# Stick-breaking mixer reordered (v in q's banks), and the second block's layer norms by token block

## The chip, the cores and the metric

The kernel runs on one core of one Trainium2 chip. The metric is the device time of one execution in microseconds (us). The kernel below ("before") took 2758.28, 2760.16 and 2761.77 us in three runs, median 2760.16 us.

## The reference

256 tokens of 1024 features go through two blocks in float32. The first has two layers of FFN, mixer, FFN and gate; its mixer is stick-breaking attention in layer 0 and a pooling mixer in layer 1. The second has two layers of mixer, layer norm, PEER (each token's 128 of 16,384 experts), layer norm; its mixer is MLA in layer 0 and DSA (attention over keys that an indexer picks) in layer 1.

```python
def stick_breaking_attention(h, w_qkv, q_gain, k_gain, w_o):
    q, k, v = jnp.split(h @ w_qkv, 3, axis=-1)          # each 256 x 1024
    q = rms_norm(q.reshape(B, S, 16, 64), q_gain)       # per head
    k = rms_norm(k.reshape(B, S, 16, 64), k_gain)
    ...  # z = q k^T / 8; weights = exp(log_sigmoid(z) + later log_sigmoid(-z)); o = weights v
    return o @ w_o

def second_block(x, ...):
    for i in range(2):
        m = _mla_mixer(x, ...) if i == 0 else _dsa_mixer(x, ...)      # both end in o @ w_o
        x = _layernorm(DN_ALPHA * x + m, ln_gain[i, 0], ln_bias[i, 0])
        f = _peer(x, peer_w_q[i], peer_sub_keys[i], peer_w_down[i], peer_w_up[i])
        x = _layernorm(DN_ALPHA * x + f, ln_gain[i, 1], ln_bias[i, 1])
    return x
```

`_layernorm` takes mean and variance over a token's 1024 features: both column halves.

## The kernel before

**Tiling.** The tokens are two token blocks of 128 (`TB`), the features two halves of 512 columns (`HALVES`). A 256x1024 product is four parts (block, half), one PSUM bank each. `acc(0)` ("set 0") is banks 0 to 3, `acc(1)` banks 4 to 7. Weights come as units of 128x1024 (512 KB). SP loads a unit into a ring of six raw slots, ACT rounds it to `w_hi` (L655), DVE writes the rest `w_lo = raw - w_hi` (L1106), and PE makes three products for each part: high times high, high times low, low times high (L1848, L1849, L1850; `mm3`). A unit is 12 matmuls of 512 columns, a unit of the 584-wide indexer rows 6 of 512 and 6 of 72. `split(n)` on ACT or DVE is n such units; `unit_used` counts what PE has used, `hi_done` and `lo_done` what is ready. Activations are held turned (features on partitions) as `act_hi` and `act_lo` in `act_both`; PE turns rows with 128x128 transposes (L1880, L1891).

**Order.** Each engine's program is written by hand in one order, and waits are semaphores: `t.after(s)` counts the next value. `rows(set, n)` are n units into a set, `by_part` announces the last unit part by part.

**Stick-breaking mixer.** PE makes q's eight units into set 0 and k's into set 1, then turns q into banks 0 to 3 (L1880), waits until k is kept, makes v's units into set 1 and turns k after the sixth (`KEY_TURN`). ACT keeps q, k and v out of PSUM with their squares (`keep_acc`, L728). DVE scales q's and k's heads (`head_norm`, L1242), with splits after each. Then `stick_breaking` runs eight pairs of heads: logits (L1982), sums (L1991), mixing. `wo`'s eight units go to set 0.

**Layer norm of the second block.** `layer_norm` on DVE: four residual adds out of PSUM that also sum (L1351), a mean after each second (L1357), then for each block: wait for ACT's square (L831), variance (L1116), POOL's power (L488), scale by halves (L1372, two of 128x512). PE turns eight 128x128 per block; ACT scales the turned rows into `xT` and copies to `act_hi`, DVE subtracts into `act_lo` (L1140, `turned_ln`). Gain and bias are put on `x` itself later, by two DVE instructions per block: behind the experts' norm by `finish_x` (L1378, L1379), one split after the turning.

**Places.** The layer norm stands behind MLA's `wo` (before PEER's queries), behind the experts' down products (before DSA's indexer rows), behind DSA's `wo` (before the gather) and at the end; in the first two its last adds wait for the parts of the last unit, and a split stands behind it. Behind DSA's `wo` ACT squares both blocks first, then turns block 0 (`turned_whole`), block 0's first queries and scores follow on PE (`first_block`), DVE ranks them (L1566), and the gather begins.

**POOL's queue.** In layer 0 POOL scatters gates by 256 indirect DMAs (L544) and brings them back. In layer 1 it loads `pad` (gain and bias), makes the last 16 of the 128 copies of 512 KB that fill `both_rows` in DRAM (L567; both stand behind `x_changed(TB)`, a wait for both blocks of `finish_x`), and then gathers 256 times (L583); DVE takes the dot products (L1739), PE the weighted sums (L2294). SP's loads are queue q1 of the profile, POOL's q0.

## Time and profile before

| | us |
|---|---|
| median of three runs | 2760.16 (2758.28 to 2761.77) |
| the profiled execution | 2757.85 |
| its span | 2756.0 |
| PE busy | 2542.8 (92%) |
| DVE busy | 2062.0 (75%) |
| ACT busy | 1279.2 (46%) |
| POOL busy | 1147.6 (42%) |

The mean granted TensorE clock was 0.985 of full. Busy shares are averages over stages with different limits.

### The profile page before, as it was taken

The page shows a single profiled execution, that of the slowest core. Times are in us where ns is not written, and L with a number is a line of the kernel's source. Part 1 is how long each engine was busy: PE and PEld are TensorE (multiplying, and loading weights), DVE is VectorE, ACT ScalarE, POOL GpSimd, SP SyncE. Part 2 cuts the span into 40 slices and gives each one's busy share as a digit, 9 for nine tenths or more (in the row PEclk, how much of TensorE's full clock was granted, in tenths as well). Part 3 has the DMA queues.
Part 4 walks back from the last instruction along what each step waited for, and adds up shares of the span by engine and source line. Part 5 has one row for each costly group of instructions (what it writes and reads, how often), then busy time and mean ns, then how long its engine had stood idle before and what let it go on. Part 6 is the DMA issues. An engine that isn't in the chain of part 4 may idle for free.

```text
span 2756.0 us, 38867 instructions
## 1 busy us (share of the span) xinstructions
PE 2542.8 (92%) x12724; PEld 1980.0 (72%) x12724; DVE 2062.0 (75%) x4122; ACT 1279.2 (46%) x2160; POOL 1147.6 (42%) x1482
## 2 busy tenths in 40 slices
PE   8999899999999999999999899999987888887777
PEld 7887688878888877899999788887765333433223
DVE  7886588788878876798999567666777776777675
ACT  5555555555555555555555445455443222222222
POOL 4443044344434411388787533331103444444443
PEclk9999999999999999999999999999999999999998
DMA  9996799889979966455556799997938999999998
GB/s 356 379 320 211 283 384 373 279 328 377 324 264 383 368 222 218 153 175 182 183 180 198 250 382 389 383 385 285 314 129 341 422 416 422 412 422 419 414 411 341
DMA packets 217832, 873.30 MB, mean 317 GB/s; under 512 B 38320, under 2 KB 38448, under 8 KB 184048
## 3 DMA queue, kind: packets, MB, share of 16 engines
q0 software_dynamic: 118496, 511.47, 47.6%
q1 hardware_dynamic: 99072, 359.38, 37.0%
q10 hardware_dynamic: 144, 1.05, 0.1%
q8 instruction: 51, 0.84, 0.1%
q14 instruction: 69, 0.57, 0.1%
HBM read 786.70 MB, written 152.17 MB: 341 GB/s over the span
## 4 chain that ended last, share of the span: by engine, by line
PE 50%; DMA 21%; POOL 12%; DVE 7%; issue 5%; ACT 3%; SPq 0%; DVEq 0%; POOLq 0%; ACTq 0%
PE ps L1931 12%; DMA arena<-both_rows,arena 11%; POOL gate_cells L544 11%; PE ps L1848 8%; PE ps L1849 8%; PE ps L1850 8%; DMA both_rows<-in_stream 8%; PE ps L2294 6%; PE ps L1933 6%; DVE arena L1739 2%; PE ps L2251 1%; DMA raw<-in_stream 1%; DVE w_lo L1106 1%; PE ps L2032 1%; ACT w_hi L655 1%
## 5 line engine op out<-in xcount | busy, mean ns | idle before, releaser
L1106 DVE TENSOR_TENSOR w_lo<-raw,w_hi 128x1024 fp32r<-128x1024 f32 x665 | 811.0, 1223 | 290.4 <-ACT w_hi L655 285.8
L655 ACT ACTIVATE w_hi<-raw 128x1024 fp32r<-128x1024 f32 x665 | 701.8, 1058 | 461.0 <-DMA raw<-in_stream 316.3
L2294 PE MATMUL ps<-arena 128*128 128x512 f32 x1024 | 483.1, 620 | 126.5 <-ACT arena L872 126.4
L1931 PE MATMUL ps<-act_both,w_hi 128*128 128x512 f32 x1408 | 502.3, 399 | 6.6 <-DVE act_both L1134 4.8
L2294 PEld LDWEIGHTS ps<-arena 128*128 128x128 f32 x1024 | 192.8, 196 | 406.1 <-ACT arena L872 204.4
L1739 DVE SCALAR_TENSOR_TENSOR arena<-arena 128x1024 f32<-128x1024 f32 x256 | 313.6, 1225 | 186.6 <-DMA arena<-both_rows,arena 184.9
L583 POOL DMA_INDIRECT arena<-both_rows,arena x256 | 290.5, 1135 | 369.5 <-PE ps L2294 342.5
L516 POOL DMA_DIRECT2D both_rows<-arena x512 | 280.1, 554 | 353.1 <-DVE arena L1183 343.4
L1848 PE MATMUL ps<-w_hi,act_both 128*128 128x512 f32 (+1 forms) x990 | 386.0, 390 | 26.1 <-DVE w_lo L1106 12.8
L1933 PE MATMUL ps<-act_both,w_lo 128*128 128x256 f32 x1408 | 394.8, 280 | 0.0
L1849 PE MATMUL ps<-w_lo,act_both 128*128 128x512 f32 (+1 forms) x990 | 383.0, 387 | 0.0
L1850 PE MATMUL ps<-w_hi,act_both 128*128 128x512 f32 (+1 forms) x990 | 382.5, 387 | 0.0
L544 POOL DMA_INDIRECT gate_cells<-hot x256 | 316.0, 1235 | 110.2 <-issue 83.2
L1848 PE MATMUL ps<-act_both,w_hi 128*128 128x256 f32 x1192 | 339.5, 285 | 3.6 <-DVE act_both L1140 1.5
L1849 PE MATMUL ps<-act_both,w_hi 128*128 128x256 f32 x1192 | 338.0, 284 | 0.0
L1850 PE MATMUL ps<-act_both,w_lo 128*128 128x256 f32 x1192 | 337.9, 283 | 0.0
L1931 PEld LDWEIGHTS ps<-act_both,w_hi 128*128 128x128 f32 x1408 | 264.5, 188 | 74.9 <-issue 4.5
L1933 PEld LDWEIGHTS ps<-act_both,w_lo 128*128 128x128 f32 x1408 | 265.8, 189 | 3.0
L865 ACT ACTIVATE hot<-hot 128x2 f32<-128x2 f32 (+1 forms) x132 | 26.8, 203 | 458.3 <-DVE arena L1739 457.5
L1848 PEld LDWEIGHTS ps<-w_hi,act_both 128*128 128x128 f32 x990 | 188.1, 190 | 69.6 <-DVE w_lo L1106 12.0
L1848 PEld LDWEIGHTS ps<-act_both,w_hi 128*128 128x128 f32 x1192 | 229.4, 192 | 5.1 <-issue 3.8
L1849 PEld LDWEIGHTS ps<-act_both,w_hi 128*128 128x128 f32 x1192 | 229.5, 193 | 0.0
(276 smaller groups left out, 3652.8 us busy)
## 6 DMA issues: line engine op xcount, KB each, us to landing
raw<-in_stream SPq DMA_DIRECT2D x675, 512.0 KB, 3.4
arena<-in_stream POOLq DMA_DIRECT2D x128, 512.0 KB, 9.7
both_rows<-arena POOLq DMA_DIRECT2D x512, 128.0 KB, 6.3
both_rows<-in_stream POOLq DMA_DIRECT2D x128, 512.0 KB, 7.0
gate_cells<-hot POOLq DMA_DIRECT2D x32, 512.0 KB, 21.2
hot<-gate_cells POOLq DMA_DIRECT2D x128, 128.0 KB, 7.0
gate_cells<-hot POOLq DMA_INDIRECT x256
arena<-both_rows,arena POOLq DMA_INDIRECT x256, 10.8
```

Source lines behind the costliest of these rows:

```text
L516: pool.dma_start(rows.rearrange("(c r) k -> r c k", r=32), arena[32 * a:32 * a + 32, A_RELAY_OUT + UNIT * s:A_RELAY_OUT + UNIT * s + UNIT] ...
L544: pool.indirect_dma_start(gate_cells[:, :], bass.IndirectOffsetOnAxis(ap=cell[:, q:q + 1], axis=0), weights[:, q:q + 1], None).then_inc(sc ...
L583: pool.indirect_dma_start(row[:, p % ROW_RING, :], None, both_rows[:, :], at).then_inc(row_in[p % ROW_RING], 16)
L655: act.activation(w_hi[:, u % SPLIT, :], raw[:, u % RAW, :], ACT.Copy).then_inc(hi_done, 1)
L1106: dve.tensor_tensor(w_lo[:, u % RAW, :], raw[:, u % RAW, :], w_hi[:, u % SPLIT, :].bitcast(F32), ALU.subtract).then_inc(lo_done, 1)
L1739: dve.scalar_tensor_tensor(row[:, p % ROW_RING, 0:D], row[:, p % ROW_RING, 0:D], 1.0, x_rows[:, b, :], ALU.mult, ALU.mult, accum_out=dots[ ...
L1848: pe.matmul(dst, lhs[0], rhs[0], start=first, stop=False, **kw)
L1849: pe.matmul(dst, lhs[0], rhs[1], start=False, stop=False, **kw)
L1850: return pe.matmul(dst, lhs[1], rhs[0], start=False, stop=last, **kw)
L1931: pe.matmul(ps[:, bank, :], high, act_both[:, :, k, :], start=k == 0, stop=k == KD - 1, skip_group_check=True)
L1933: ins = pe.matmul(ps[:, bank, T:2 * T], low, act_hi[:, k, :], start=False, stop=k == KD - 1, skip_group_check=True)
L2294: ins = pe.matmul(ps[:, 2 * (n % 2) + half, :], diags[:, p % DIAG_RING, :], row[:, p % ROW_RING, D + 512 * half:D + 512 * half + 512], sta ...
```

## The change

In the stick-breaking mixer v's units stand directly behind k's and go to q's banks (set 0), the turns of q and k go to banks 4 to 7 and stand after v's second and seventh unit (`QUERY_TURN`, `KEY_TURN`), the pairs' banks are turned by four, and `wo` and the norm behind it change sets. ACT and DVE have two units fewer ahead of the pairs and two more among them.

In three of the four layer norms the last units (`TAIL` two, `DSA_TAIL` three behind DSA's `wo`) are made part by part rather than unit by unit (`last_units`): all of block 0 first. `layer_norm` on DVE starts block 0's variance before block 1's last add. Behind MLA's `wo`, ACT scales straight into `act_hi`, and DVE computes `xT` again from PSUM. Behind the experts, the first pair of turned features and the first two indexer units go by token block too, splits stand between the pairs, and `finish_x` is cut in two `finish_block`s: one five splits later, one behind the indexer's rope and two more splits. On POOL `x_changed(TB)` moves from behind the last `norm()` of layer 0's gates to ahead of `pad`'s load, with all of the layer's copies behind it that stood behind it before.

-KEY_TURN = 5
+QUERY_TURN, KEY_TURN = 1, 6
...
+TAIL, DSA_TAIL = 2, 3
@@ -609,6 +611,7 @@
         if i == 1:
+            x_changed(TB)
             pool.dma_start(pad[:, :], lnc[2 * i]).then_inc(ln_in, 16)
@@ -631,7 +634,6 @@
         norm()
-        x_changed(TB)
@@ -685,17 +687,36 @@
+    def scaled_pair(dst, n, pair, lo, hi):
+        act.wait_ge(turned, t.after(turned))
+        for k in (2 * pair, 2 * pair + 1):
+            g = G_LN + 2 * KD * n + k
+            ins = act.activation(dst[:, k, lo:hi], ps[:, 4 + pair, (k % 2) * T + lo:(k % 2) * T + hi],
+                                 ACT.Identity, scale=cst[:, g:g + 1], bias=cst[:, g + KD:g + KD + 1])
+        return ins
     def turned_ln(n):
...
+        for pair in range(4):
+            scaled_pair(act_hi, n, pair, 0, T).then_inc(turned_hi, 1)
+    def pair_high(pair, lo=0, hi=T):
+        both = slice(2 * pair, 2 * pair + 2)
+        act.activation(act_hi[:, both, lo:hi], xT[:, both, lo:hi], ACT.Copy).then_inc(turned_hi, 1)
...
+    def turned_ln_apart(n):
+        scaled_pair(xT, n, 0, 0, P).then_inc(first_pair_read, 1)
+        act.wait_ge(first_pair_read, 1)
+        pair_high(0, 0, P)
+        split()
+        step(scaled_pair(xT, n, 0, P, T))
+        pair_high(0, P, T)
+        for pair in range(1, 4):
+            step(scaled_pair(xT, n, pair, 0, T))
+            pair_high(pair)
+            split(2 if pair == 2 else 1)
@@ -803,6 +824,8 @@
             if p + 2 < N_PAIRS:
                 softplus(p + 2)
+            else:
+                split()
@@ -908,14 +931,14 @@
             keep_acc(q_tok, 0, roots=1)
-            split(KD)
-            keep_acc(k_tok, 1, roots=1)
-            keep_turned(area(A_QT, 2048), range(4), cst[:, QG:QG + 1])
-            split(KEY_TURN + 1)
-            keep_turned(area(A_KT, 2048), range(4), cst[:, KG:KG + 1])
+            split(KD - 1)
+            keep_acc(k_tok, 1, roots=1, pending=1)
+            split(3)
+            keep_turned(area(A_QT, 2048), range(4, 8), cst[:, QG:QG + 1])
+            split(KD - SPLIT)
+            keep_turned(area(A_KT, 2048), range(4, 8), cst[:, KG:KG + 1])
             act.preload_act_table_set("natural_log_exp_and_others")
-            split(KD - KEY_TURN - 1)
-            keep_acc(v_tok, 1, roots=1)
+            keep_acc(v_tok, 0, roots=1, pending=2)
@@ -1013,7 +1036,7 @@
-            split(KD)
+            split(KD - 3)
             keep_acc(tok(S_I, 584), 0, 584)
@@ -1035,19 +1058,18 @@
             split(KD - SPLIT)
-            layer_norm()
+            layer_norm([0])
             turned_whole(2 * i, 0)
+            layer_norm([1])
             first_block()
             turned_whole(2 * i, 1)
             gathered()
             layer_norm([1])
...
-        split(KD - 1)
+        split(KD - TAIL)
         layer_norm()
-        split()
         turned_ln(2 * i)
+        split(TAIL)
@@ -1082,9 +1104,8 @@
-        split(RING - 1)
+        split(RING - TAIL)
         layer_norm()
-        split()
@@ -1134,11 +1155,33 @@
+    def pair_low(pair, lo=0, hi=T):
+        both = slice(2 * pair, 2 * pair + 2)
+        dve.tensor_tensor(act_lo[:, both, lo:hi], xT[:, both, lo:hi], act_hi[:, both, lo:hi].bitcast(F32),
+                          ALU.subtract).then_inc(act_ready, 1)
+    def turned_ln(n):
+        for pair in range(4):
             dve.wait_ge(turned_hi, t.after(turned_hi))
-            dve.tensor_tensor(act_lo[:, 2 * b:2 * b + 2, :], xT[:, 2 * b:2 * b + 2, :],
-                              act_hi[:, 2 * b:2 * b + 2, :].bitcast(F32), ALU.subtract).then_inc(act_ready, 1)
+            for k in (2 * pair, 2 * pair + 1):
+                g = G_LN + 2 * KD * n + k
+                ins = dve.tensor_scalar(xT[:, k, :], ps[:, 4 + pair, (k % 2) * T:(k % 2) * T + T],
+                                        cst[:, g:g + 1], cst[:, g + KD:g + KD + 1], ALU.mult, ALU.add)
+            step(ins)
+            pair_low(pair)
+    def first_low():
+        dve.wait_ge(turned_hi, t.after(turned_hi))
+        pair_low(0, 0, P)
+    def turned_ln_apart():
+        split()
+        dve.wait_ge(turned_hi, t.after(turned_hi))
+        pair_low(0, P, T)
+        for pair in range(1, 4):
+            dve.wait_ge(turned_hi, t.after(turned_hi))
+            pair_low(pair)
+            split(2 if pair == 2 else 1)
@@ -1357,31 +1402,45 @@
+    def layer_norm(pending=1, first_at_once=False, between=None):
+        def summed(n):
             b, c = part(n, pending)
             residual(b, n % HALVES, c)
-            if n % HALVES == HALVES - 1:
-                mean(b)
-        dve.wait_ge(mean_ready, t.after(mean_ready, TB))
-        for b in range(TB):
+        def variance_of(b):
             dve.wait_ge(stat_ready, t.after(stat_ready))
-            inverse_root(b, small[:, 4 + b:5 + b], LN_EPS)
+            dve.tensor_scalar(small[:, b:b + 1], small[:, 4 + b:5 + b], 1.0 / D, LN_EPS, ALU.mult,
+                              ALU.add).then_inc(var_ready, 1)
+        def scale(b, between=None):
+            dve.wait_ge(mean_ready, t.after(mean_ready))
+            dve.wait_ge(rstd_ready, t.after(rstd_ready))
             for h in range(HALVES):
                 dve.tensor_scalar(x[:, b, half(h)], x[:, b, half(h)], small[:, 12 + b:13 + b],
                                   small[:, 16 + b:17 + b], ALU.add, ALU.mult).then_inc(rows_ready, 1)
+                if h == 0 and between is not None:
+                    between()
+        summed(0)
+        summed(1)
+        mean(0)
+        summed(2)
+        variance_of(0)
+        if first_at_once:
+            scale(0)
+        summed(3)
+        mean(1)
+        if not first_at_once:
+            scale(0)
+        variance_of(1)
+        scale(1, between)
-    def finish_x():
-        t.after(ln_in, 16)
@@ -1393,14 +1452,14 @@
             stick_terms()
-            head_norm(q_tok, 1.0, HD * EPS)
-            head_norm(k_tok, 1.0 / HD, EPS)
+            head_norm(q_tok, 1.0, HD * EPS, KD - 6)
+            head_norm(k_tok, 1.0 / HD, EPS, 2)
             t.skip(acc_kept)
...
                 b, c = part(n, 1)
-                dve.tensor_tensor(x[:, b, c], acc(0)[:, b, c], x[:, b, c], ALU.add).then_inc(x_ready, 1)
+                dve.tensor_tensor(x[:, b, c], acc(1)[:, b, c], x[:, b, c], ALU.add).then_inc(x_ready, 1)
@@ -1471,7 +1528,9 @@
-            split(KD)
+            split(KD - 3)
+            t.after(ln_in, 16)
+            finish_block(0, ln_in, t.value(ln_in))
@@ -1484,7 +1543,9 @@
             dve.tensor_copy(kid[:, :, IDX:P], kid[:, :, 0:IDX]).then_inc(rows_ready, 1)
-            split(KD)
+            split(2)
+            finish_block(1, ln_in, t.value(ln_in))
+            split(KD - 2)
@@ -1529,12 +1590,12 @@
             split(KD - SPLIT)
-            layer_norm(pending=SPLIT)
+            layer_norm(pending=SPLIT, first_at_once=True)
         else:
-            split(KD - 1)
-            layer_norm()
-            turned_ln()
-            split()
+            split(KD - TAIL)
+            layer_norm(pending=TAIL)
+            turned_ln(2 * i)
+            split(TAIL)
@@ -1828,8 +1889,8 @@
-        split(RING - 1)
-        layer_norm()
+        split(RING - TAIL)
+        layer_norm(TAIL, between=first_low)
@@ -1855,9 +1916,9 @@
+    def rows(set_, n_units, n=D, fresh=True, at=0, then={}, by_part=None, late=(), tail=0, skip=0):
...
             if k in then:
                 then[k]()
+        last_units([(at + k, unit()) for k in range(n_units - tail, n_units)], by_part, set_)
+    def last_units(pairs, by_part, set_=0, **kw):
+        for b in range(TB if pairs else 0):
+            for h in range(HALVES):
+                for n, (k, s) in enumerate(pairs):
+                    ins = mm3(ps[:, 4 * set_ + 2 * b + h, :], a(k, P * b, P), w(s, 512 * h, 512), False,
+                              n == len(pairs) - 1, **kw)
+                    if (b, h) == (TB - 1, HALVES - 1):
+                        ins.then_inc(unit_used, 1)
+                if (b, h) != (TB - 1, HALVES - 1):
+                    ins.then_inc(by_part, 1)
@@ -1886,6 +1960,8 @@
     def turn_block(b):
         for k in range(KD):
+            if (b, k) == (0, KD - HALVES):
+                pe.wait_ge(mean_ready, TB * (2 * DEPTH - 1))
             if k % (KD // HALVES) == 0:
@@ -1912,6 +1988,29 @@
+    def turn_first_pair_apart():
+        for b in range(TB):
+            for k in range(KD):
+                if k % (KD // HALVES) == 0:
+                    pe.wait_ge(rows_ready, t.after(rows_ready))
+                if (b, k) == (1, 0):
+                    pe.wait_ge(first_pair_read, 1)
+                ins = pe.transpose(ps[:, 4 + k // 2, T * (k % 2) + P * b:T * (k % 2) + P * b + P],
+                                   x[:, b, P * k:P * k + P], ident)
+                if k == 1 or (b and k % 2):
+                    ins.then_inc(turned, 1)
+    def first_units_apart(n):
+        s = [unit() for _ in range(TAIL)]
+        for b in range(TB):
+            pe.wait_ge(act_ready, t.after(act_ready))
+            for k in range(TAIL):
+                for lo in range(0, n, 512):
+                    m = min(512, n - lo)
+                    ins = mm3(ps[:, 2 * b + lo // 512, 0:m], a(k, P * b, P), w(s[k], lo, m), k == 0, False)
+                if b:
+                    ins.then_inc(unit_used, 1)
@@ -2071,20 +2170,22 @@
+            def turn_queries():
+                pe.wait_ge(acc_kept, t.after(acc_kept))
+                pe.wait_ge(rows_ready, t.after(rows_ready))
+                turn_rows(q_tok, range(4, 8))
             def turn_keys():
                 pe.wait_ge(rows_ready, t.after(rows_ready))
                 pe.wait_ge(turned_kept, t.after(turned_kept, 4))
-                turn_rows(k_tok, range(4))
+                turn_rows(k_tok, range(4, 8))
             rows(0, KD)
             rows(1, KD, fresh=False)
             pe.wait_ge(acc_kept, t.after(acc_kept))
-            pe.wait_ge(rows_ready, t.after(rows_ready))
-            turn_rows(q_tok, range(4))
-            pe.wait_ge(acc_kept, t.after(acc_kept))
-            rows(1, KD, fresh=False, then={KEY_TURN: turn_keys})
+            rows(0, KD, fresh=False, then={QUERY_TURN: turn_queries, KEY_TURN: turn_keys})
             stick_breaking()
-            rows(0, KD, fresh=False, by_part=part_done, late=(KD - 2, KD - 1))
+            rows(1, KD, fresh=False, by_part=part_done, late=(KD - 2, KD - 1))
@@ -2211,7 +2312,8 @@
-            rows(0, KD, 584)
+            first_units_apart(584)
+            rows(0, KD, 584, skip=TAIL)
@@ -2225,7 +2327,7 @@
-        rows(0, KD, fresh=False, by_part=part_done)
+        rows(0, KD, fresh=False, by_part=part_done, tail=DSA_TAIL if i else TAIL)
@@ -2352,22 +2454,23 @@
                 expert_down(j % RING)
-        for j in range(NK % TURN):
-            expert_down(j % RING, j == NK % TURN - 1)
+        for j in range(NK % TURN - TAIL):
+            expert_down(j % RING)
+        pe.wait_ge(eh_ready, t.after(eh_ready, TAIL))
+        last_units([(j % RING, unit()) for j in range(NK % TURN - TAIL, NK % TURN)], part_done,
+                   skip_group_check=True)

The instructions on the engines, in two places (a row is an instruction or a run of equal ones: line, operation, output and inputs, shape; numbers left out).

PE in the stick-breaking mixer, from the last two products of k's eighth unit (before): `arena` holds q's scaled rows, L1880 is the turn, the rows behind it are v's first unit.

```order
L1849 MATMUL ps<-w_lo,act_both 128x512
L1850 MATMUL ps<-w_hi,act_both 128x512
L1880 MATMUL ps<-cst,arena 128x128 [waits rows_ready,acc_kept]
L1880 MATMUL ps<-cst,arena 128x128 x15
L1848 MATMUL ps<-w_hi,act_both 128x512 [waits lo_done,acc_kept]
L1849 MATMUL ps<-w_lo,act_both 128x512
```

The same in the new program, from the last two products of v's second unit; the turn is L1954 and the products L1909 to L1911.

```order
L1910 MATMUL ps<-w_lo,act_both 128x512
L1911 MATMUL ps<-w_hi,act_both 128x512
L1954 MATMUL ps<-cst,arena 128x128 [waits rows_ready,acc_kept]
L1954 MATMUL ps<-cst,arena 128x128 x15
L1909 MATMUL ps<-w_hi,act_both 128x512 [waits lo_done]
L1910 MATMUL ps<-w_lo,act_both 128x512
```

The turn stands two units later, and the product behind it no longer waits for what is kept.

DVE behind the experts' norm, from its last scale, before: L1372 scales `x`, L1140 makes the low halves of the turned rows, L1378 and L1379 are `finish_x`.

```order
L1372 TENSOR_SCALAR x<-x,small 128x512 [waits rstd_ready]
L1372 TENSOR_SCALAR x<-x,small 128x512
L1140 TENSOR_TENSOR act_both<-arena,act_both 128x512 [waits turned_hi] x4
L1106 TENSOR_TENSOR w_lo<-raw,w_hi 128x1024 [waits hi_done]
L1378 TENSOR_TENSOR x<-x,pad 128x1024 [waits ln_in]
L1379 TENSOR_TENSOR x<-x,pad 128x1024 [waits dve_step]
L1378 TENSOR_TENSOR x<-x,pad 128x1024 [waits ln_in]
L1379 TENSOR_TENSOR x<-x,pad 128x1024 [waits dve_step]
L1106 TENSOR_TENSOR w_lo<-raw,w_hi 128x1024 [waits hi_done] x8
```

And now (L1420 the scale, L1160 the low halves, L1127 the split, L1442 and L1443 `finish_block`):

```order
L1420 TENSOR_SCALAR x<-x,small 128x512 [waits rstd_ready,mean_ready]
L1160 TENSOR_TENSOR act_both<-arena,act_both 128x2x128 [waits turned_hi]
L1420 TENSOR_SCALAR x<-x,small 128x512
L1127 TENSOR_TENSOR w_lo<-raw,w_hi 128x1024 [waits hi_done]
L1160 TENSOR_TENSOR act_both<-arena,act_both 128x2x128 [waits turned_hi]
L1160 TENSOR_TENSOR act_both<-arena,act_both 128x512 [waits turned_hi]
L1127 TENSOR_TENSOR w_lo<-raw,w_hi 128x1024 [waits hi_done]
L1160 TENSOR_TENSOR act_both<-arena,act_both 128x512 [waits turned_hi]
L1127 TENSOR_TENSOR w_lo<-raw,w_hi 128x1024 [waits hi_done] x2
L1160 TENSOR_TENSOR act_both<-arena,act_both 128x512 [waits turned_hi]
L1127 TENSOR_TENSOR w_lo<-raw,w_hi 128x1024 [waits hi_done] x6
L1442 TENSOR_TENSOR x<-x,pad 128x1024 [waits ln_in]
```

Five splits stand ahead of four of the eight that followed `finish_x`; only block 0 is finished behind them, and block 1 comes behind the rope and two more splits.

## Rows read from the trace of the kernel before

**Rows 1.** The page's chain that ended last, by line.

```profile
PE ps L1931 12%; DMA arena<-both_rows,arena 11%; POOL gate_cells L544 11%; PE ps L1848 8%; PE ps L1849 8%; PE ps L1850 8%; DMA both_rows<-in_stream 8%; PE ps L2294 6%; PE ps L1933 6%; DVE arena L1739 2%; PE ps L2251 1%; DMA raw<-in_stream 1%; DVE w_lo L1106 1%; PE ps L2032 1%; ACT w_hi L655 1%
```

**Rows 2.** Windows: length; busy PE, PEld, DVE, ACT, POOL (instructions); PEclk; DMA share; GB/s.

```profile
1600.00:1700.00 100.00, 100.00 (x443) 82.84 (x442) 69.43 (x112) 50.44 (x74) 34.74 (x65) 1.00 1.01 386
1935.00:1937.00 2.00, 2.00 (x7) 1.73 (x8) 2.00 (x3) 0.00 (x0) 0.03 (x1) 0.54 0.92 269
1935.00:2000.00 65.00, 63.35 (x305) 52.04 (x306) 46.31 (x62) 31.19 (x38) 8.38 (x17) 0.97 0.94 318
2072.00:2074.00 2.00, 1.83 (x8) 1.86 (x9) 0.88 (x2) 2.00 (x7) 0.00 (x0) 0.50 1.02 412
2092.00:2756.00 664.00, 529.57 (x1274) 236.43 (x1272) 460.20 (x1243) 158.43 (x475) 287.98 (x255) 0.97 0.99 408
```

**Rows 3.** Timeline, stick-breaking mixer: start, duration, engine, line; idle before, and releaser.

```profile
247.11 1.91 PE L1880 MATMUL ps<-cst,arena 128*128 128x128 f32 x16
250.48 0.50 PE L1848 MATMUL ps<-w_hi,act_both 128*128 128x512 f32 x1 [1.47 <-ACT arena L728]
...
269.05 3.34 PE L1880 MATMUL ps<-cst,arena 128*128 128x128 f32 x16 [1.95 <-DVE arena L1242]
...
278.06 0.71 PE L1982 MATMUL ps<-arena 64*128 64x256 f32 x4
...
279.19 2.10 ACT L728 ACTIVATE arena<-ps,small 128x1024 f32<-128x1024 f32 x2
...
285.03 0.91 PE L1991 MATMUL ps<-arena 128*128 128x384 f32 x2 [2.01 <-DVE arena L1274]
```

**Rows 4.** Timeline, the norm behind MLA's wo, and the first scatter.

```profile
1112.29 0.39 PE L1850 MATMUL ps<-w_hi,act_both 128*128 128x512 f32 x1
...
1115.84 1.15 ACT L831 ACTIVATE arena<-x,small 128x1024 f32<-128x1024 f32 x1 [0.48 <-DVE small L1357]
...
1116.68 1.00 DVE L1372 TENSOR_SCALAR x<-x,small 128x512 f32<-128x512 f32 x2 [0.69 <-POOL small L488]
...
1118.42 1.00 DVE L1372 TENSOR_SCALAR x<-x,small 128x512 f32<-128x512 f32 x2 [0.68 <-POOL small L488]
...
1122.30 0.55 PE L1848 MATMUL ps<-act_both,w_hi 128*128 128x256 f32 x1 [1.31 <-DVE act_both L1140]
...
1146.12 1.19 POOL L544 DMA_INDIRECT gate_cells<-hot  x1 [27.03 <-DVE hot L1702]
```

**Rows 5.** Timeline, the norm behind the experts, the indexer's rows and the first copy.

```profile
1913.09 0.39 PE L1850 MATMUL ps<-w_hi,act_both 128*128 128x512 f32 x1
...
1923.01 0.50 PE L1848 MATMUL ps<-w_hi,act_both 128*128 128x512 f32 x1 [1.30 <-DVE act_both L1140]
...
1928.73 1.22 DVE L1378 TENSOR_TENSOR x<-x,pad 128x1024 f32<-128x1024 f32 x1
...
1934.88 0.54 PE L1848 MATMUL ps<-w_hi,act_both 128*128 128x512 f32 x1 [3.47 <-DVE w_lo L1106]
...
1937.33 1.07 POOL L567 DMA_DIRECT2D both_rows<-in_stream  x2 [2.31 <-issue]
...
1944.54 0.28 PE L1850 MATMUL ps<-w_hi,act_both 128*128 128x72 f32 x1
```

**Rows 6.** The last copy's issue, and SP's queue in 1935 to 2000: packets, MB, share.

```profile
1993.19 0.52 POOL L567 DMA_DIRECT2D both_rows<-in_stream  x1 [5.06 <-DMA both_rows<-in_stream]
q1 hardware_dynamic: 2948, 10.75, 47.5%
```

**Rows 7.** The page's DMA issues: KB each, us from issue to landing.

```profile
gate_cells<-hot POOLq DMA_DIRECT2D x32, 512.0 KB, 21.2
```

**Rows 8.** Timeline, the norm behind DSA's wo, and the first gather.

```profile
2067.36 0.39 PE L1850 MATMUL ps<-w_hi,act_both 128*128 128x512 f32 x1
...
2070.75 1.16 PE L1891 MATMUL ps<-cst,x 128*128 128x128 f32 x8 [3.00 <-DVE x L1372]
...
2086.40 1.19 POOL L583 DMA_INDIRECT arena<-both_rows,arena  x1 [14.56 <-DVE arena L1649]
```

248 lines of the change are left out of this document (169 added, 79 removed).

## The prediction, made before the changed kernel was timed

> **What bounds the kernel now.** I read the chain that ended last first [rows 1]. Its named PE lines (L1931, L1848 to L1850, L1933, L2294) make 48%, POOL's scatter (L544) and the gather's DMA 11% each. So time is saved where PE stands still in front of its next product and nothing else is late behind it. The windows come second [rows 2]. In 1600 to 1700 PE made 443 matmuls of 512 columns or their like in 100.00 us and was never idle: 0.226 us each, 2.71 us for a unit of twelve. In 2092 to 2756 the DMA share is 0.99 at 408 GB/s: the gather is bound by DMA, and it starts earlier or later as a block. Last came the timelines of the four places that the diff touches [rows 3, 4, 5, 8]: where PE waits, for whom, and how far the next engine is behind.
>
> The sum is made against the profiled execution: 2757.85 us, span 2756.0. The median is 2760.16, 2.3 more, which is added at the end.
>
> **Stick-breaking mixer [rows 3].** Before, k's products end at 247.11. Then come 1.91 of turning q, 1.47 of waiting until k is kept, v's first six units, 1.95 of waiting for k's norm on DVE, a turn of 3.34 instead of 1.91, and two units. The pairs begin at 278.06. The first sums begin at 285.03, 6.97 later, at the end of a chain of ACT and DVE: ACT starts to keep v only at 279.19, 1.1 late, behind a split.
> After: v's eight units stand directly behind k's, because they go to banks that q has left. Eight units and two turns give 247.11 + 8 x 2.72 + 2 x 1.91 = 272.7. The turns wait for nothing: the first stands two units later, when k must be kept (k is out of PSUM by 250.5, the turn at 252.6), the second at 268.1, where k's norm, ready at 269.05 before, must be ready. That norm's chain on DVE stands one split earlier than before (two fewer ahead of the pairs in all, one of them ahead of it; at 1.23 us this makes 267.8), so it is nearly a tie; if it is late, it costs about 1. The pairs begin 5.4 earlier. Keeping v loses its 1.1 behind the split and a further 0.4, so the sums follow 5.5 later: 278.2 instead of 285.03. Gain 6.8. The two splits that move into the last two pairs lie beside PE's mixing; what they push back there is bounded by 2 x 1.23 = 2.5, and I take 0 because the norm of `wo`'s units has weights in six slots. Bounds: 4 and 8.
>
> **Norm behind MLA's wo [rows 4].** PE's last part is ready at 1112.68. Four adds and two means, begun there, take until about 1115.84, when ACT squares block 1 (1.15) and DVE turns to block 0's variance; 0.84 later, behind POOL's power, scale 0 starts (1116.68), then scale 1 at 1118.42, and the first product comes 3.88 after that, at 1122.30. By parts, two units of three products each, the four parts are ready 6 x 0.226 = 1.36 apart: 1108.6, 1110.0, 1111.3, 1112.7. So three adds are done by then, and one add with its mean remains (3.55 for four and two; I take 1.1): 1113.8. Scale 0 runs then, its variance being ready. The square of block 1 takes 1.15 and a hand-over of some 0.3, variance and power 0.84: scale 1 at 1116.1 instead of 1118.42. Gain 2.3. The turned rows lose one ACT copy on the way to `act_hi`, and DVE gets two scalings out of PSUM per pair in front of `act_lo`. No row shows this form; the nearest is half a scale pair, L1372, 0.50 each, for the same 512 columns. One pair of 256 columns beside ACT's work costs between -0.5 (the copy was longer) and 1.0 (two such rows). I take 0.3, nearer to the copy saved. Gain 2.0. It is passed on to POOL's first scatter (1146.12), which has waited 27.03 us for DVE's ranking, and that engine's chain is at PE's back until the experts begin. Bounds: 1 and 3.
>
> On this form the Trainium skill (VectorE: DVE Perf Modes, "Why PSUM operands drop a tier") says that an f32 operand in PSUM caps the engine at its slowest mode. No row here has the same operation from both memories; by the rule the two scalings would cost more than from SBUF, and the gain here would be nearer to 1 than to 2.
>
> **Norm behind the experts [rows 5].** Here all three delays of PE are attacked. From the last product's start at 1913.09 to the first indexer product at 1923.01 it takes 9.92. As above scale 1 comes 2.3 earlier. `first_low` between the halves of scale 1 and the turning of block 0's first pair in advance let PE begin with block 0 of two units once two transposes, one ACT pair and one DVE subtraction are done: I take 1919.2, a gain of 3.8. Between 1923.01 and 1931.41 (1934.88 less the stall of 3.47) lie four units of the indexer's rows, 2.1 each. Then PE waits 3.47 at 1934.88 for `w_lo`, because `finish_x` (four instructions of 1.22 from 1928.73, L1378 and L1379) holds DVE's splits. Now these stand behind five more splits, and nothing holds PE's fifth unit: gain 3.47. After that stall the granted clock was 0.54 in 1935 to 1937 [rows 2], that is 1.2 GHz for most of it, and the last four units took 9.8, to 1944.7, instead of 8.4: gain 1.4. Together 8.7. Against it, the first products now come in two halves behind a pause of PE, and more of them at the lower level: 0.4 lost. Gain 8.3: the indexer's rows end at 1936.4 instead of 1944.7. Bounds: 4.5 and 9.5.
>
> **The copies.** `finish_block(1)` ends at about 1948 to 1950 (eleven splits and a rope on DVE's way), and the 16 copies wait for it. They were issued from 1937.33 to 1993.19 [rows 5, 6], 3.7 us each. From 1951 they last until about 2010. In 1935 to 2000 the DMA engines are busy at 0.94, 318 GB/s [rows 2]; 10.75 MB of it are SP's units [rows 6], the other 9.9 MB the copies. So PE's q, k and v units now run first without the copies, then beside them later. The amount of work is the same and the ring of six units gains a lead first: I take 0. Nobody but the gather wants the copies, and it starts at 2083.
>
> **Norm behind DSA's wo [rows 8].** PE's last product starts at 2067.36; its turn of block 0 at 2070.75, 3.00 idle. With three units by parts the parts are ready 9 x 0.226 = 2.03 apart: 2061.6, 2063.7, 2065.7, 2067.75. Block 0 has its mean at 2064.8. From the start of a square to its block's scale it took 2.58 behind MLA's wo (1115.84 to 1118.42) [rows 4]: scale 0 at 2067.4, before block 1's last add. PE turns when the first half is scaled, 0.50 and a hand-over of 0.1 later: 2068.0, gain 2.8, and ACT no longer squares block 1 ahead of turning block 0, 0.5. Gain 3.3; the first gather goes out at 2083.1 instead of 2086.40, and all behind it with it. Bounds: 2 and 4.
>
> **Sum.** 6.8 + 2.0 + 8.3 + 3.3 = 20.4. 2757.85 - 20.4 = 2737.4; with 2.3 to the median, 2739.8: I say 2740.
>
> **Rivals.**
> (a) The copies starve q, k and v. For it: both queues are full [rows 2, 6]. In 1951 to 2010 SP's units get an equal half of 318 GB/s or so, 10.75 MB in 65 us, 165 GB/s. Then 512 KB take 3.17 us and PE wants one per 2.71; over 19 units 8.7 are lost. Against it: before, the same two flows ran side by side with PE 63.35 busy of 65. Time 2749. Chance 0.13.
> The Trainium skill (DMA: Bandwidth & Descriptors, the table row "Inside each SDMA engine") has each engine go round-robin between the queues; the trace agrees with 10.75 against about 9.9 MB. By this rule, (a) is what happens if SP's ring has no lead, and the time is the 2749 above.
> (b) Some of the moves don't arrive: k's norm comes after its turn, and the first products behind two norms run at the lower clock level. A stall of 1 to 2 and a turn of 3.34 for 1.91 in the mixer, 3 less behind the experts, the low bounds elsewhere: 4 + 1 + 4.5 + 2 = 11.5. Time 2749. Chance 0.09.
> (c) Slower: the gather waits for the copies. Its place is POOL's wait for the last copy ahead of L583. If a copy took as long as the slowest 512 KB transfer on this queue, 21.2 from issue to landing with two in flight [rows 7], that is 10.6 each: 1951 + 16 x 10.6 = 2121, 38 after 2083, so 2775. It decides from 8.2 us per copy; before they took 3.7. Chance 0.02.
> (d) It does nothing that counts: the scatter's and the gather's chains give back what PE gains, as each has its own pace [rows 1]. Time 2760. Chance 0.04. Against it: both start on what PE's chain hands them [rows 4, 8].
> (e) More than I add up: no stall is left in DSA's rows and the clock stays up. Time 2735. Chance 0.12.
>
> **How the numbers follow.** The forecast itself 0.60. A measurement of this kernel tells 0.2%, 5.5 us, from no change. Faster: the forecast, (e), (a), (b), 0.94; same: (d), 0.04; slower: (c), 0.02. The range: the high bounds sum to 8 + 3 + 9.5 + 4 = 24.5 (2735.7), and with (e) some stalls more, 2732; above, it includes (a) and (b) at 2749 with 2 for their own spread: 2751.
>
> **What would show it.** In the new trace: v's products end near 270 and the pairs begin at 272.7 with no idle time before either turn; the first sums near 278; scale 1 behind MLA's wo 2.3 earlier relative to PE's last part; no L1127 stall of PE between 1919 and 1937 and PEclk near 1 there; copies from about 1951 to 2010 (all minus the gain so far) and PE still over 0.97 busy beside them; PE's turn behind DSA's wo within 1 us of its last product. I'm wrong if PE's idle time in q, k and v grows by over 3 us, or if the first gather follows the last copy and not the ranking.

## The result and the profile after

The changed kernel took 2734.56 us (median of six, 2729.83 to 2744.22), the kernel before 2760.27 beside it: ratio 0.992, interval 0.9904 to 0.9937. Its profiled execution took 2735.61, span 2733.8 (2756.0 before), 22.2 less; 20.4 were forecast. The interval leaves out 1, so the gain of 0.8% is clear of the noise. Measured once more in another session, the same kernel gave 2736.94 against 2754.94, ratio 0.9928 (0.9915 to 0.9941), span 2735.8.

The page after: the span, the clock line and the chain by line (L2030 was L1931, L1909 to L1911 were L1848 to L1850, L546 was L544).

```profile
span 2733.8 us, 38880 instructions
...
PEclk9999999999999999999999999999999999999999
...
DMA arena<-both_rows,arena 12%; PE ps L2030 12%; POOL gate_cells L546 12%; PE ps L1909 11%; PE ps L1910 10%; PE ps L1911 10%; PE ps L2032 6%; PE ps L2396 6%; DVE arena L1800 2%; DMA raw<-in_stream 1%; PE ps L2353 1%; ACT w_hi L657 1%; PE ps L2131 1%; DVE w_lo L1127 1%; ACT act_both L686 1%
```

The DMA of the copies, 8% of the chain in [rows 1], is gone from it, and the products have taken its place. The chain only names one way back through work that ran side by side; what moved is read from the timelines.

Timeline of the stick-breaking mixer after, to be set beside [rows 3] (start, duration, engine, line):

```profile
252.68 1.91 PE L1954 MATMUL ps<-cst,arena 128*128 128x128 f32 x16
...
262.39 2.28 DVE L1285 TENSOR_TENSOR arena<-arena,small 128x2048 f32<-128x2048 f32 x1
...
268.06 1.91 PE L1954 MATMUL ps<-cst,arena 128*128 128x128 f32 x16
...
272.64 0.71 PE L2081 MATMUL ps<-arena 64*128 64x256 f32 x4
...
272.74 2.12 ACT L749 ACTIVATE arena<-ps,small 128x1024 f32<-128x1024 f32 x2 [0.32 <-PE ps L1911]
...
278.20 0.91 PE L2090 MATMUL ps<-arena 128*128 128x384 f32 x2 [1.61 <-DVE arena L1317]
```

Both turns take 1.91 and have no idle time in front, the pairs begin at 272.64 (forecast 272.7), ACT keeps v 0.1 later rather than 1.1, and the sums begin at 278.20 (forecast 278.2). k's norm ends at 264.67, 3.4 before its turn, where 0.3 was forecast. The forecast counted the one split fewer ahead of it as DVE's 1.23. But before, these splits waited for work too:

```profile
262.85 1.23 DVE L1106 TENSOR_TENSOR w_lo<-raw,w_hi 128x1024 fp32r<-128x1024 f32 x1 [1.49 <-ACT w_hi L655]
265.57 1.23 DVE L1106 TENSOR_TENSOR w_lo<-raw,w_hi 128x1024 fp32r<-128x1024 f32 x1 [1.49 <-ACT w_hi L655]
266.71 2.28 DVE L1242 TENSOR_TENSOR arena<-arena,small 128x2048 f32<-128x2048 f32 x1
```

They come 2.72 apart, the pace of PE's units, so a split fewer ahead of the norm is worth 2.72 and not 1.23.

Timeline behind MLA's `wo` after, beside [rows 4]:

```profile
1105.22 0.39 PE L1911 MATMUL ps<-w_hi,act_both 128*128 128x512 f32 x1
...
1106.75 1.00 DVE L1420 TENSOR_SCALAR x<-x,small 128x512 f32<-128x512 f32 x2
...
1106.86 1.15 ACT L854 ACTIVATE arena<-x,small 128x1024 f32<-128x1024 f32 x1 [1.28 <-DVE small L1402]
...
1109.03 1.11 DVE L1420 TENSOR_SCALAR x<-x,small 128x512 f32<-128x512 f32 x2 [0.75 <-POOL small L490]
...
1110.47 3.76 ACT L695 ACTIVATE act_both<-ps,cst 128x256 fp32r<-128x256 f32 x8 [2.38 <-PE ps L1979]
1111.53 0.99 DVE L1168 TENSOR_SCALAR arena<-ps,cst 128x256 f32<-128x256 f32 x2 [1.39 <-ACT act_both L695]
1112.56 0.69 DVE L1160 TENSOR_TENSOR act_both<-arena,act_both 128x512 fp32r<-128x512 f32 x1
...
1113.40 0.55 PE L1909 MATMUL ps<-act_both,w_hi 128*128 128x256 f32 x1 [1.68 <-DVE act_both L1160]
...
1137.87 1.19 POOL L546 DMA_INDIRECT gate_cells<-hot  x1 [28.40 <-DVE hot L1763]
```

Scale 1 starts 3.42 behind the end of `wo` (1105.61) instead of 5.74 behind 1112.68: the forecast 2.3. From there to the first product it takes 4.37 instead of 3.88, 0.5 more (0.3 forecast): DVE's two scalings out of PSUM take 0.99. From ACT's first scaling to the first product it takes 2.92 instead of 2.55; that 0.37 is the new form's, the other 0.1 passes before ACT begins.

Timeline behind the experts after, beside [rows 5]: the experts' last product, the first and the last of the indexer's rows, and the turn of q in the DSA stage. In the second fence stand windows there (length; busy PE, PEld, DVE, ACT, POOL with instructions; PEclk; DMA share; GB/s):

```profile
1903.72 0.39 PE L1911 MATMUL ps<-w_hi,act_both 128*128 128x512 f32 x1
...
1909.86 0.78 PE L1909 MATMUL ps<-w_hi,act_both 128*128 128x512 f32 x1
...
1926.67 0.28 PE L1911 MATMUL ps<-w_hi,act_both 128*128 128x72 f32 x1
...
2001.77 1.96 PE L1954 MATMUL ps<-cst,arena 128*128 128x128 f32 x16 [2.04 <-ACT arena L749]
```

```profile
1908.00:1910.00 2.00, 1.76 (x9) 1.69 (x9) 2.00 (x4) 1.69 (x4) 0.00 (x0) 0.50 0.64 181
1910.00:1912.00 2.00, 2.00 (x9) 1.71 (x9) 0.70 (x3) 1.97 (x5) 0.00 (x0) 0.71 0.07 22
1912.00:1914.00 2.00, 2.00 (x13) 1.77 (x12) 1.74 (x2) 1.97 (x4) 0.00 (x0) 1.00 0.00 0
1915.00:1917.00 2.00, 2.00 (x14) 1.76 (x13) 1.75 (x3) 2.00 (x4) 0.00 (x0) 1.00 0.86 297
1945.00:2000.00 55.00, 54.30 (x262) 43.85 (x260) 47.73 (x79) 26.91 (x32) 8.28 (x16) 1.00 0.95 331
```

The first indexer product comes 5.8 behind the experts' end instead of 9.5, the eight units take 17.1 instead of 21.8 without one stop, and beside the copies PE is busy 54.30 of 55. The first units still ran at the low clock level (0.50 and 0.71 in 1908 to 1912), the rest at full clock.

Timeline behind DSA's `wo` after, beside [rows 8]:

```profile
2047.73 0.39 PE L1911 MATMUL ps<-w_hi,act_both 128*128 128x512 f32 x1
2047.74 1.00 DVE L1420 TENSOR_SCALAR x<-x,small 128x512 f32<-128x512 f32 x2 [0.74 <-POOL small L490]
2048.34 0.90 PE L1967 MATMUL ps<-cst,x 128*128 128x128 f32 x6 [0.23 <-DVE x L1420]
...
2049.79 0.44 PE L1967 MATMUL ps<-cst,x 128*128 128x128 f32 x2 [0.55 <-DVE small L1402]
...
2063.30 1.20 POOL L585 DMA_INDIRECT arena<-both_rows,arena  x1 [9.63 <-DVE arena L1710]
```

PE turns 0.23 behind its last product instead of 3.00.

### The profile page after: what moved, and what is told of

The parts are those of the page before. It is cut to its first block, busy times and chain, and to the rows that moved or that the text cites. A ratio compares the mean times of both kernels' runs of the same rounds, so it can differ in the third digit from the quotient of the medians.

```text
span 2733.8 us, 38880 instructions
## 1 busy us (share of the span) xinstructions
PE 2538.3 (93%) x12724; PEld 1977.8 (72%) x12724; DVE 2065.3 (76%) x4131; ACT 1274.7 (47%) x2159; POOL 1151.2 (42%) x1482
## 3 DMA queue, kind: packets, MB, share of 16 engines
q10 hardware_dynamic: 144, 1.05, 0.1%
## 4 chain that ended last, share of the span: by engine, by line
PE 58%; DMA 14%; POOL 12%; DVE 7%; issue 5%; ACT 3%; SPq 0%; DVEq 0%; POOLq 0%; ACTq 0%
DMA arena<-both_rows,arena 12%; PE ps L2030 12%; POOL gate_cells L546 12%; PE ps L1909 11%; PE ps L1910 10%; PE ps L1911 10%; PE ps L2032 6%; PE ps L2396 6%; DVE arena L1800 2%; DMA raw<-in_stream 1%; PE ps L2353 1%; ACT w_hi L657 1%; PE ps L2131 1%; DVE w_lo L1127 1%; ACT act_both L686 1%
## 5 line engine op out<-in xcount | busy, mean ns | idle before, releaser
L1127 DVE TENSOR_TENSOR w_lo<-raw,w_hi 128x1024 fp32r<-128x1024 f32 x665 | 811.2, 1223 | 297.1 <-ACT w_hi L657 292.6
L2030 PE MATMUL ps<-act_both,w_hi 128*128 128x512 f32 x1408 | 502.3, 399 | 6.7 <-DVE act_both L1155 4.9
L585 POOL DMA_INDIRECT arena<-both_rows,arena x256 | 296.0, 1156 | 360.0 <-PE ps L2396 337.6
L1909 PE MATMUL ps<-w_hi,act_both 128*128 128x512 f32 (+1 forms) x990 | 384.9, 389 | 17.6 <-DVE w_lo L1127 7.2
L1911 PE MATMUL ps<-w_hi,act_both 128*128 128x512 f32 (+1 forms) x990 | 382.4, 387 | 0.0
L546 POOL DMA_INDIRECT gate_cells<-hot x256 | 316.6, 1237 | 111.0 <-issue 82.6
L1909 PE MATMUL ps<-act_both,w_hi 128*128 128x256 f32 x1192 | 340.0, 285 | 3.0 <-DVE act_both L1160 1.7
L1911 PE MATMUL ps<-act_both,w_lo 128*128 128x256 f32 x1192 | 338.2, 284 | 0.0
L2030 PEld LDWEIGHTS ps<-act_both,w_hi 128*128 128x128 f32 x1408 | 264.5, 188 | 75.0 <-issue 4.5
L1909 PEld LDWEIGHTS ps<-act_both,w_hi 128*128 128x128 f32 x1192 | 229.7, 193 | 4.7 <-issue 3.4
L1909 PEld LDWEIGHTS ps<-w_hi,act_both 128*128 128x128 f32 x990 | 187.9, 190 | 58.6 <-DVE w_lo L1127 9.2
```

Of the source, the lines that this page charges most:

```text
L546: pool.indirect_dma_start(gate_cells[:, :], bass.IndirectOffsetOnAxis(ap=cell[:, q:q + 1], axis=0), weights[:, q:q + 1], None).then_inc(sc ...
L585: pool.indirect_dma_start(row[:, p % ROW_RING, :], None, both_rows[:, :], at).then_inc(row_in[p % ROW_RING], 16)
L1127: dve.tensor_tensor(w_lo[:, u % RAW, :], raw[:, u % RAW, :], w_hi[:, u % SPLIT, :].bitcast(F32), ALU.subtract).then_inc(lo_done, 1)
L1909: pe.matmul(dst, lhs[0], rhs[0], start=first, stop=False, **kw)
L1911: return pe.matmul(dst, lhs[1], rhs[0], start=False, stop=last, **kw)
L2030: pe.matmul(ps[:, bank, :], high, act_both[:, :, k, :], start=k == 0, stop=k == KD - 1, skip_group_check=True)
```

## The stretches of all kernels

Each number is the distance between two landmarks in one trace, in us. *B*: end of MLA's `wo` to first product, and to first scatter. *X*: first scatter to the experts' last product. *D*: from there to the first indexer product, and to the turn of q. *E*: start of DSA's `wo` to the first gather. *G*: first gather to the end of the span.

| kernel | sums at | B | X | D | E | G | span | ratio to before |
|---|---|---|---|---|---|---|---|---|
| before | 285.03 | 9.63, 33.45 | 767.35 | 9.54, 107.48 | 40.71 | 669.6 | 2756.0 | 1 |
| changed | 278.20 | 7.80, 32.27 | 766.23 | 5.76, 97.67 | 37.34 | 670.5 | 2733.8 | 0.992 |
| changed again | 277.60 | 7.79, 32.38 | 769.38 | 5.76, 97.47 | 37.36 | 669.9 | 2735.8 | 0.9928 |
| e1 mixer only | 276.87 | 9.63, 33.43 | 767.44 | 9.53, 106.95 | 40.43 | 670.6 | 2748.9 | 0.9973 |
| e2 norms only | 282.80 | 7.79, 32.47 | 767.90 | 5.34, 96.09 | 37.32 | 670.4 | 2736.1 | 0.9945 |
| e3 old turning | 277.24 | 7.41, 31.22 | 765.07 | 5.76, 98.64 | 37.34 | 669.1 | 2727.8 | 0.9926 |
| e4 finish early | 277.34 | 7.54, 31.55 | 767.59 | 5.77, 98.14 | 37.31 | 670.9 | 2733.8 | 0.9930 |
| e5 whole first units | 277.34 | 7.43, 31.88 | 767.98 | 7.08, 104.05 | 37.33 | 673.5 | 2744.0 | 0.9927 |
| e6 tails of one | 277.44 | 10.50, 34.51 | 769.08 | 8.47, 99.50 | 40.31 | 670.0 | 2739.2 | 0.9955 |
| e9 sums first | 277.41 | 8.17, 32.48 | 768.72 | 6.15, 100.01 | 40.26 | 670.8 | 2741.3 | 0.9946 |
| e10 8 copies | 277.23 | 7.90, 31.91 | 767.50 | 5.75, 96.79 | 37.33 | 668.7 | 2728.7 | 0.9923 |
| e7 32 copies | 277.81 | 7.53, 32.85 | 759.86 | 5.69, 102.04 | 38.47 | 670.9 | 2733.2 | 0.9905 |
| e11 24, 72, 32 copies | 276.91 | 8.41, 32.22 | 759.55 | 5.33, 100.16 | 38.60 | 669.7 | 2725.1 | 0.9913 |
| e12 24, 64, 40 copies | 277.68 | 7.48, 31.29 | 758.30 | 5.34, 100.26 | 56.40 | 672.9 | 2747.5 | 0.9976 |

The first product behind either norm repeats within 0.5 among kernels with the same instructions there (except e11's 8.41), and E within 0.3 where no copies run beside it; stretches beside heavy DMA spread by 1 to 4 (X by 4 among kernels that have the same instructions in it). So a place is judged by its stretch and the whole by its ratio.

## Experiments

**The two halves of the change apart.** e1 is the kernel before with the mixer's hunks alone, e2 the changed kernel without them.

```diff
 # e1 against before
-KEY_TURN = 5
+QUERY_TURN, KEY_TURN = 1, 6
...
-                    rows(1, KD, fresh=False, then={KEY_TURN: turn_keys})
+                    rows(0, KD, fresh=False, then={QUERY_TURN: turn_queries, KEY_TURN: turn_keys})
```

> The kernel before with the stick-breaking part alone (v in q's banks, turns to banks 4 to 7, wo's set, two splits among the pairs); the second block is as before. Theory 1, the places add up: the first sums behind the logits come 6.8 us earlier than before (285.03 becomes 278.2), PE's idle of 1.47 and 1.95 in front of v and of the key turn and the slow turn of 3.34 are gone, all that follows lies 6.9 earlier, and the kernel takes about 6.9 us less than before (ratio 0.9975). Rival, given back: weights, the experts' DMA-bound stage (share 1.00) or the gather take up the slack, and the end moves by under 3 us.

> The changed kernel with the stick-breaking part as before; only the second block's norms, first units and finish steps are changed. Theory 1, the places add up: 22.2 us less 6.9, so about 15.3 us faster than before (ratio 0.9945), the first product behind MLA's wo 1.9 nearer to the last of wo, the indexer's rows ending 7.7 nearer to the experts' end, the first gather 3.2 nearer to the end of DSA's wo. Rival, given back: well under 15, because the two parts used different slack.

e1: 2749.43 against 2755.31, ratio 0.9973 (0.9959 to 0.9987), 0.9975 expected. e2: 2739.12, ratio 0.9945 (0.9928 to 0.9961), 0.9945 expected. The two gains, 0.27% and 0.55%, add to 0.82%, where the whole showed 0.80% and 0.72%. Nothing is given back that these intervals, 0.3% wide, could tell. The 7.7 in e2's expectation, as the changed kernel's gain up to the end of the indexer's rows, was misread: it is 8.5 (22.85 from the experts' end instead of 31.34), and e2, whose rows ran at full clock from the first product, gains 9.4.

**The finish steps at their old place.**

```diff
                     turned_ln_apart()
+                    t.after(ln_in, 16)
+                    for b in range(TB):
+                        finish_block(b, ln_in, t.value(ln_in))
...
                     split(KD - 3)
-                    t.after(ln_in, 16)
-                    finish_block(0, ln_in, t.value(ln_in))
...
-                    split(2)
-                    finish_block(1, ln_in, t.value(ln_in))
-                    split(KD - 2)
+                    split(KD)
```

> The changed kernel with both blocks' gain and bias (four DVE instructions of 1.23 us) put back in one piece ahead of the indexer's rows, directly behind the turning; the same five splits stand ahead of it. The 16 copies then start some 20 us earlier, as before. Theory 1 (these four instructions were the 3.47 stall and the slow clock behind it): PE waits again, 2 to 3.5 us, for w_lo, with a granted clock near 0.5 for some 2 us, and the indexer's rows end 3 to 5 later than in the changed kernel. Rival (the splits between the pairs give DVE such a lead that the place of the four is free): under 0.5 us of idle, no loss. A second question: PE's waits of 1.65 and 0.81 in the q, k and v units of before come back (theory: they come from copies that start together with the indexer's rows) or not.

The one stop of PE in e4's indexer rows:

```profile
1924.60 0.50 PE L1908 MATMUL ps<-w_hi,act_both 128*128 128x512 f32 x1 [0.77 <-DVE w_lo L1127]
```

0.77, not 3.47. The rows end 24.1 behind the experts, 1.0 to 1.3 later than in the two traces of the changed kernel (22.85 and 23.15), and q's turn comes 0.5 to 0.7 later; the ratio is 0.9930 (0.9907 to 0.9953), no difference. Both theories missed, the rival by less. Before, the four instructions held DVE for 4.9 with one split between the turning and them; behind five splits the same 4.9 cost 0.77. The waits of 1.65 and 0.81 in q, k and v did not come back, nor does e1 have them (one of 0.42, with before's whole DSA stage and its early copies; the changed kernel has the same 0.42). So they belong to that one trace. Ahead of the first of them ACT had waited 4.58 for a raw unit (split at 1970.86).

**The first indexer units whole, the five splits behind the pairs, and the old turning behind MLA's wo.**

```diff
-                    turn_first_pair_apart()
+                    norm(x)
...
-                    turned_ln_apart()
+                    turned_ln(1)
+                    split(5)
...
-                layer_norm(TAIL, between=first_low)
+                layer_norm(TAIL)
...
-                    first_units_apart(584)
-                    rows(0, KD, 584, skip=TAIL)
+                    rows(0, KD, 584)
```

> The changed kernel without the early part of the first indexer units: the turning waits for all rows, ACT and DVE turn four whole pairs as in the kernel before and only then come the five splits, the first two units are made whole. The same form of turning (ACT to xT, copy, DVE subtracts) is also used behind MLA's wo. Theory 1: the first indexer product comes 1.5 later than in the changed kernel after the last expert product (7.7 instead of 6.1), and behind MLA's wo the first product comes 0.5 earlier than in the changed kernel. In all 1 us slower than the changed kernel behind the experts, less what the splits behind the pairs add: five splits of DVE in one piece do not delay PE, as four units are split ahead. Rival: PE runs out of split units, over 2 us idle in the indexer's rows.

The first product comes 1.3 later (7.08 for 5.76; 1.5 expected). Then PE runs out of split units at the third, as the rival had it, and later q's turn waits long. Timeline of e5:

```profile
1917.88 0.47 PE L1907 MATMUL ps<-w_hi,act_both 128*128 128x512 f32 x1 [2.00 <-DVE w_lo L1129]
...
2001.84 1.06 ACT L657 ACTIVATE w_hi<-raw 128x1024 fp32r<-128x1024 f32 x1 [4.66 <-DMA raw<-in_stream]
...
2006.59 1.92 ACT L750 ACTIVATE arena<-ps 128x1024 f32<-128x1024 f32 x2
```

So with `finish_x` moved away PE still stops, when all five splits stand behind the pairs: the splits between the pairs keep it going. The 2.00 is not a part of before's 3.47. In e5 two units are ready when PE begins and the third is split behind the turning; before had four ready, the fourth split directly behind the turning, and stopped at the fifth. How much each of the five brings was not tried, nor the first units whole by themselves. The second wait is another thing: ACT's next two splits stand ahead of keeping v, they wait for raw units 4.66 and 2.73 beside the last copies, and the turn behind waits 5.34. That wait was 2.04 and 1.55 in the two traces of the changed kernel and 1.29 in before, e1 and e4, whose copies were over. But it was also 3.85 in e9 and 1.29 in e6, which have the changed kernel's instructions and copies there, so it varies from trace to trace; in e9 and in e5 ACT waited over 4 for one raw unit (4.23, 4.66). The times say 0.9927 (0.9899 to 0.9956), no difference from the changed kernel; but an interval 15 us wide could not show 3.3 more in every execution either.

**The old form of turning behind MLA's wo.**

```diff
-                    scaled_pair(act_hi, n, pair, 0, T).then_inc(turned_hi, 1)
+                    step(scaled_pair(xT, n, pair, 0, T))
+                    pair_high(pair)
```

> The changed kernel with the turning behind MLA's wo in its old form: ACT scales into xT and copies to act_hi, DVE only subtracts. In the changed kernel's trace DVE needs 1.63 us per pair (two scalings out of PSUM 0.99, a subtraction 0.69) where ACT needed 1.57 per pair before, and PE's granted clock stays at 0.50 for 6 us instead of 4. Theory 1 (the new turning costs 0.7 to 1 us and eats half of the norm's gain): from the last product of wo to the first scatter 31.5 to 31.9 us instead of 32.3 (33.4 before), the kernel 0.5 us faster than the changed one, no verdict from the times. Rival (the form is neutral or better, as it frees ACT): 32.3 or more.

The first product comes 0.4 earlier (7.41, in e5 7.43, for 7.80), where 0.5 was expected of e5. In single traces the new form ranges from 7.53 to 7.90, but from ACT's first scaling to the first product it takes 2.92 in each of them and 2.55 in each of the old form: 0.37. The scatter comes 1.05 earlier in e3 but 0.4 in e5, which has the same form. The windows of 2 us from the first product on say why: granted clock 0.50, 0.67, 1.00 in e3 and 0.50, 0.50, 0.50, 0.98 in e5; in the new form 0.50, 0.50, 0.53, 1.00 (changed) and 0.50, 0.56, 1.00 (e4). How long the level of 1.2 GHz lasts is not the form's doing. Ratio 0.9926 (0.991 to 0.9943), no verdict from the times. The form costs 0.4 at the first product, and my 6 us against 4 us of slow clock as its price was wrong.

**The tails and DVE's order apart.** e6 keeps the order and sets the tails to one unit (the first indexer units that go by block stay two, and one split moves from the DSA rows to ahead of the norm); e9 keeps the tails and sums all four parts first.

```diff
 # e6
-TAIL, DSA_TAIL = 2, 3
+TAIL, DSA_TAIL, FIRST = 1, 1, 2
 # e9
                 summed(2)
+                summed(3)
+                mean(1)
                 variance_of(0)
-                if first_at_once:
-                    scale(0)
-                summed(3)
-                mean(1)
-                if not first_at_once:
-                    scale(0)
+                scale(0)
```

> The changed kernel with only the last unit made part by part in all three norms (TAIL and DSA_TAIL 1, as before); the order of the adds, means, variances and scales on DVE stays new, the first indexer units stay apart, one split more stands ahead of each of the first two norms. Theory 1 (the gain of the norms is that block 0's sums are done under PE's products, which needs the tail): of the 2 us behind MLA's wo and behind the experts each, and of the 3.2 behind DSA's wo, under a third is left; the first gather comes 2 to 3 later after DSA's wo begins (39.5 to 40.5 instead of 37.3; 40.7 before), all in all 5 us slower than the changed kernel. Rival (the order on DVE does it): within 1 us per place of the changed kernel.

> The changed kernel with DVE's order in the norms as it was before (all four adds and both means, then variance and scale of block 0, then of block 1), but with the tails part by part. Theory 1 (behind MLA's wo and the experts the tail alone does it, behind DSA's wo the early scale counts): up to 0.5 us lost at each of the first two places, 2 to 2.5 us lost behind DSA's wo (gather 39.3 to 39.8 behind wo's start instead of 37.3). Rival (the order is worth nothing, as PE has to finish its last unit anyway): within 0.5 us of the changed kernel at all three.

e6 is 2742.72 against 2754.32, 0.9955 (0.9939 to 0.9972); e9 is 2742.53 against 2754.94, 0.9946 (0.9931 to 0.996). Behind MLA's `wo` the new order without tails is worse than before (10.50 for 9.63): the turning costs 0.5 of it, the other 0.4 is block 0's variance, for which DVE waits (for ACT's square) while block 1's last part lies ready. The tails without the order keep most (8.17). Behind the experts the first indexer product comes at 8.47 without tails and at 6.15 without the order, for 5.76. (e9's D up to q's turn, 100.01, holds the 3.85 named above, which is not the order's.) Behind DSA's `wo` either alone is worth nothing, 40.31 and 40.26 of 40.71, and both together 3.4: block 0 can only be scaled under PE's products if its parts come early and DVE does not queue it behind block 1's last add, which waits for those products.

**How many copies stand beside the DSA rows.**

```diff
-COPIES_MLA, COPIES_UP = 16, 96
+COPIES_MLA, COPIES_UP = 16, 80    # e7: 32 copies in the DSA stage
+COPIES_MLA, COPIES_UP = 24, 96    # e10: 8
```

> The changed kernel with 32 instead of 16 table copies behind the finish steps in the DSA stage (16 fewer during the experts). Theory 1 (the ring of six units and the shared queues give PE what it needs nearly always; copies cost under 1 us): PE idle in the q, k and v units under 2 us, the copies end near 2055 to 2065 and the gather starts where it did, near 2063; the experts' stage, which is bound by DMA, is some 16 x 1 us shorter at most or the same. Rival (a) (copies starve the raw stream): each unit beside copies takes up to 3.17 instead of 2.72, so some 4 to 8 us more idle time of PE between 1945 and 2050 than in the changed kernel; and the last copy holds the gather if a copy takes over 3.6 us.

> The changed kernel with 8 instead of 16 copies in the DSA stage and 24 instead of 16 in MLA's stage, where POOL waits 30.55 us before its power. Theory 1 (in the changed kernel the copies end at 2003, beside v's last units: ACT waits for raw units 20.3 us in ten of 22 splits, and q's turn waits 2.04 instead of 1.29): with 8 copies, over by about 1975, that wait is 1.29 again, and the stage from the experts' end to q's turn is 0.7 to 1 us shorter. Rival (the copies are hidden): no change. The first scatter may come later if the eight copies more run into POOL's power behind MLA's wo (more than 32.3 from the end of wo's products).

With 8, q's turn waits 1.29 and D is 0.7 to 0.9 shorter, as expected, and the first scatter is not held (31.91); ratio 0.9923. With 32, PE stops beside them, the longest for 2.40:

```profile
1957.91 0.50 PE L1909 MATMUL ps<-w_hi,act_both 128*128 128x512 f32 x1 [2.40 <-DVE w_lo L1127]
```

D takes 102.04, 4.4 more, and E 1.1 more (PE waits 0.99 for `w_lo` once in `wo`'s units). After the stop the clock is at the low level for some 3 us. So rival (a)'s mechanism exists, but needs the longer run of copies. The experts' stage pays it back: X is 759.86, 6.4 and 9.5 less than in the two traces of the changed kernel and 5.2 less than in any trace with 96 copies. The ratio is 0.9905 (0.9888 to 0.9921); its interval overlaps with those of the changed kernel and of e3 and e10, which were measured beside it, so a gain over them is likely and not shown by the times. Windows over the experts' down products, with 96 copies (changed) and with 80 (e7):

```profile
1545.00:1904.00 359.00, 353.11 (x1536) 291.39 (x1536) 239.86 (x387) 174.65 (x254) 116.72 (x219) 0.99 0.99 373
1545.00:1896.00 351.00, 349.90 (x1532) 288.81 (x1532) 239.66 (x384) 172.20 (x252) 108.04 (x202) 0.99 0.97 356
```

PE stands still for 5.9 us with 96 copies and for 1.1 with 80. What could be had there by moving copies is nearly gone with the first 16.

**Versions that could beat both.** The old turning, 24 copies in MLA's stage, and 72 (e11) or 64 (e12) beside the experts, so 32 or 40 in the DSA stage.

> The changed kernel once more, unaltered, so that the versions beside it are compared with it on one chip, and to see how far its stages vary from trace to trace. Expected: ratio to before 0.991 to 0.993; the norms' stretches the same within 0.3 us (wo's end to the first indexer product 5.3 to 5.8, gather 37.3 behind wo's start), the stretches beside the copies and the experts' stage spread by 1 to 2 us. If q's turn waits 2.04 us for ACT again, the wait is the order's; if it waits 1.29 as before the change, it was this one trace's DMA.

> A version that could beat both: the changed kernel with the old form of turning behind MLA's wo, 24 copies in MLA's stage, 72 beside the experts, 32 in the DSA stage. Theory 1 (the experts' stage is bound by DMA, 24 copies of 512 KB fewer there save up to 24 x 0.45 = 11 us; the copies in the DSA stage cost 4 to 6 us there, the turning gives 0.5 to 1): 5 to 6 us faster than the changed kernel. Rival (the experts' stage has another bound, PE, from 334.9 us on, its busy time being 335 of 336 in the version with 80 copies): the further 8 copies save nothing, 2 to 3 us faster than the changed kernel.

> The same with 64 copies beside the experts and 40 in the DSA stage. Theory 1: the experts' stage is at PE's pace already with 80 copies (335 us), so eight fewer save nothing; the last copy is issued 8 x 2.5 us later than with 32, near 2048, and lands by 2053, just ahead of the first gather at 2055: the same time as with 72 and 32. Rival: the copies now hold the gather, and the first gather follows the last copy instead of DVE's ranking, 2 to 10 us slower than with 32.

On one chip: changed again 2736.94, e11 2729.80, ratio 0.9913 (0.9899 to 0.9927), e12 2749.27, ratio 0.9976 (0.9967 to 0.9985). e11 is the fastest there, by 7.1 of the median; its interval overlaps with that of the changed kernel. Eight copies more moved into the DSA stage (40 for 32) cost it all. The last of them in e12:

```profile
2055.93 0.52 POOL L569 DMA_DIRECT2D both_rows<-in_stream  x1 [3.68 <-DMA both_rows<-in_stream]
2056.43 0.55 POOL L624 DMA_DIRECT2D arena<-in_subkeys  x1
2057.00 0.58 POOL L490 TENSOR_TENSOR small<-small,cst 128x1 f32<-128x1 f32 x1
```

and who waits:

```profile
2057.68 1.00 DVE L1416 TENSOR_SCALAR x<-x,small 128x512 f32<-128x512 f32 x2 [18.10 <-POOL small L490]
...
2058.29 2.13 PE L1963 MATMUL ps<-cst,x 128*128 128x128 f32 x8 [17.59 <-DVE x L1416]
```

The gather was not held by the last copy's landing, as I and rival (c) had it. POOL's power for the norm behind DSA's `wo` stands in its queue behind the issue of the copies, and each issue waits for the copy two before it. The last eight issues, from 2031.33 on, came 3.5 apart, where 2.5 had been reckoned; in 2043 to 2057 PE did nothing at all, with the DMA share at 1.02. The power comes 38.8 behind the start of `wo`, in e11 22.4. In e11 the last issue is at 2027.19, the first gather at 2055.37.

## Why the prediction was right, point by point

The time and the range held, 2734.56 for 2740 (2732 to 2751), and so did the sum against the span: 20.4 forecast, 22.2 and 20.2 measured. By place the first trace has 6.8 in the mixer, 1.2 up to the scatter, 9.8 up to q's turn, 3.4 behind DSA's `wo`; the other 1.0 lies in stretches that the change doesn't touch and that spread by more than that. So the sum held in part by luck: one place gave less than forecast, one more.

- **Mixer, 6.8:** 6.83 in the changed kernel's trace, and alone (e1) a ratio of 0.9973 where 6.9 us are 0.9975. The margin of k's norm was mis-sized, 3.4 instead of 0.3: a split ahead of it is worth PE's 2.72 and not DVE's 1.23.
- **Norm behind MLA's wo, 2.0:** 1.83 at the first product, 1.1 to 1.2 at the scatter. Scale 1 came the forecast 2.3 earlier; the turning cost 0.5 for 0.3. Up to the scatter another 0.6 went to a third window at 1.2 GHz, which other traces of the same form (e4, e10) don't have.
- **Norm behind the experts, 8.3:** 3.78 to the first product (3.8 forecast), 4.7 in the rows (4.5), 8.5 to their end (8.3), 8.2 in the second trace. The 0.4 for the low clock level was about right: e2, whose rows had none of it, takes 0.5 less for them. To q's turn it is 9.8 and 10.0 less than in before, 9.3 and 9.5 less than in e1; the 1.3 beyond the rows is that before's trace had waits of 1.65 and 0.81 in q, k and v, where e1 and the changed kernel have 0.42, less the longer wait at the turn. The size held, but the cause of the 3.47 was put in the wrong place: "these stand behind five more splits" was taken as the move of `finish_x`. e4 puts that back behind the five splits and loses 1.0 to 1.3 at the rows' end and 0.5 to 0.7 at q's turn; e5 leaves it moved, gathers the splits behind the pairs, and PE stops for 2.0. So most of the gain is the lead of split units, won by splits that stand between the turned pairs.
- **Copies, 0:** with 16 copies PE is busy 54.30 of 55 us beside them. What they cost shows once, at q's turn: nothing to 0.75 in most traces, 2.6 in e9's. That the stage stayed so close to 0 was taken without a row for the ring's lead; e7 shows where it ends.
- **Norm behind DSA's wo, 3.3:** 3.37 and 3.35.
- **The rivals.** (a) was wrong for 16 copies and half right for 32: 4.4 for the 16 more, of the 8.7 that (a) had reckoned for 19 units. The Trainium skill's rule (DMA: Bandwidth & Descriptors, table row "Inside each SDMA engine") on going round between queues fits the shares beside the copies (48.6% for POOL's queue, 45.7% for SP's in 1945 to 2000), but the ring's lead covered 16 copies. (c) has its mechanism at another place (e12): POOL's power, 17.6 us ahead of the gather. (d) did not occur, nor (b), but for the low clock level at the first products behind the norms. The median fell on (e)'s 2735, and no stall over 0.42 was left in DSA's rows but the wait at q's turn; but e1 has as few stalls in q, k and v without the change, and the clock was low at the first units, so (e)'s reason for a greater gain is not the change's.
- On PSUM operands (the Trainium skill, VectorE: DVE Perf Modes, "Why PSUM operands drop a tier": an f32 operand in PSUM holds DVE at its slowest mode): DVE took 0.50 for 256 columns out of PSUM, and the same 0.50 for 512 columns from SBUF (L1420). The trace agrees with the rule; it cost 0.4 here, since ACT's copy was saved. The gain "nearer to 1 than to 2" that the prediction drew from it did not come at the first product (1.83).

## What to carry to other kernels

Split the last units of a product by output part only together with the order of the engine that consumes the parts: one without the other was worth nothing behind DSA's `wo` (0.4 of 3.4), and behind MLA's the order without the parts was worth less than nothing, while the parts alone gave 1.5 of 1.8. When a stall is read as "that long step stands in front", count how many prepared units stand ahead of it first: putting small steps between others gave most of what moving the long one was credited with. Before work is put in a queue for its bandwidth, look at which short instruction stands behind it: 8 copies stopped PE for 17.6 us by holding one power of 0.58.

## What the runs showed of the hardware that was not expected

The low clock level behind the norm of MLA's `wo` lasted two or three windows of 2 us from the first product on, with the same instructions and first products within 0.02 of each other: 0.50, 0.67, 1.00 in e3 and 0.50, 0.50, 0.50, 0.98 in e5. From the first product to the first scatter e3 takes 23.8 and e5 24.5, so two traces of one stretch differ by 0.65 us; the new form has 24.0 (e4, e10) and 24.5 (changed) in the same way. In the experts' stage (DMA share 0.99) the part of X from the first down product on, which holds the copies, took 359.2 and 359.9 in the changed kernel's traces (357.9 to 361.9 in all with 96 copies), 352.7 with 80 copies, 350.3 with 72 and 351.1 with 64: the first 16 taken away gave about 7, the next 16 about 2. With 64 PE was busy 345.00 of 345. With 24 copies in MLA's stage, e11's adds began 1 later behind `wo` (first product 8.41), e10's and e12's did not.
